# Two more seven-product pairs in the second feed-forward network, and three modulation columns moved into its first down stage

## What is computed

```python
def swiglu(h, w_gu, w_down):
    g, u = jnp.split(h @ w_gu, 2, axis=-1)
    return (jax.nn.silu(g) * u) @ w_down
...
    mod = cond @ mod_w[i] + mod_b[i]
    sh1, sc1, g1, sh2, sc2, g2, sh3, sc3, g3 = jnp.split(mod, 9, axis=-1)
    h = modulate(rms_norm(x), sh1, sc1)
    x = x + 0.5 * g1[:, None, :] * swiglu(h, ffn1_w_gu[i], ffn1_w_down[i])
...
    x = x + 0.5 * g3[:, None, :] * swiglu(h, ffn2_w_gu[i], ffn2_w_down[i])
```

## Time and profile before

| | |
|---|---|
| time, median of 3 runs | 1944.03 us (1943.16 to 1944.99) |
| profiled execution, its own time | 1943.51 us |
| its span, first to last instruction | 1941.7 us |
| busy: PE, weight loads, DVE, ACT, POOL | 98%, 86%, 73%, 47%, 11% |
| DMA, mean over the span | 136 GB/s |
| granted PE clock, mean | 0.999 |

### The profile page before, as it was taken

The page is one execution under the profiler, slowest core; times in us unless marked ns, Lnnn a source line. Parts: engine busy times, 40 slices in busy tenths (PEclk is TensorE's granted clock), DMA queues, the critical chain, the costliest instruction groups (busy, mean ns, idle before and its releaser), DMA issues.

```text
span 1941.7 us, 28004 instructions
## 1 busy us (share of the span) xinstructions
PE 1912.3 (98%) x10860; PEld 1674.0 (86%) x10860; DVE 1426.2 (73%) x2144; ACT 915.1 (47%) x1454; POOL 211.8 (11%) x245
## 2 busy tenths in 40 slices
PE   6999999999999999999999999999999999999998
PEld 5888888878888889999888998978888889899897
DVE  7664564689868798897888988876554478578485
ACT  5322222454645426446543553655565556346264
POOL 4110100016730120000011000001111000000000
PEclk9999999999999999999999999999999999999999
DMA  8665562323143583533357544333223232423232
GB/s 332 232 216 173 195 205 98 103 82 100 33 142 104 201 291 130 195 122 100 96 195 242 171 141 140 103 94 115 87 81 105 60 98 78 129 84 123 77 100 75
DMA packets 76397, 264.64 MB, mean 136 GB/s; under 512 B 8897, under 2 KB 11073, under 8 KB 76274
## 3 DMA queue, kind: packets, MB, share of 16 engines
q1 hardware_dynamic: 55296, 190.34, 30.0%
q0 software_dynamic: 20256, 72.02, 11.0%
q10 hardware_dynamic: 722, 0.61, 0.1%
HBM read 260.66 MB, written 2.13 MB: 135 GB/s over the span
## 4 chain that ended last, share of the span: by engine, by line
PE 91%; DVE 4%; issue 1%; DMA 1%; POOL 1%; ACT 1%; SPq 0%; DVEq 0%; ACTq 0%; POOLq 0%
PE bank L1827 20%; PE bank L1832 20%; PE bank L1828 20%; PE bank L1908 9%; PE bank L1907 9%; PE bank L1909 8%; DVE arena L1183 1%; PE bank L2310 1%; PE bank L2327 1%; PE bank L2242 1%; PE bank L2086 1%; DMA arena<-in_mod_t_dram 1%; DVE h_lo L1363 1%; PE bank L2088 1%; PE bank L2087 1%
## 5 line engine op out<-in xcount | busy, mean ns | idle before, releaser
L1827 PE MATMUL bank<-h_hi,whi 128*128 128x512 f32 x1008 | 400.2, 397 | 5.3 <-ACT h_hi L751 2.8
L1828 PE MATMUL bank<-h_hi,wlo 128*128 128x512 f32 x1008 | 394.3, 391 | 0.0
L1832 PE MATMUL bank<-h_lo,whi 128*128 128x512 f32 x1008 | 347.5, 391 | 2.2 <-POOL h_lo L531 2.1
L634 ACT ACTIVATE whi<-wraw 128x1024 fp32r<-128x1024 f32 x238 | 247.5, 1053 | 181.7 <-PE bank L1832 164.7
L1827 PE MATMUL bank<-hid_hi,whi 128*128 128x512 f32 (+1 forms) x856 | 328.8, 384 | 0.0
L1828 PE MATMUL bank<-hid_hi,wlo 128*128 128x512 f32 (+1 forms) x856 | 328.1, 383 | 0.0
L1832 PE MATMUL bank<-hid_lo,whi 128*128 128x512 f32 (+1 forms) x856 | 328.0, 383 | 0.0
L1096 DVE TENSOR_TENSOR wlo<-wraw,whi 128x1024 fp32r<-128x1024 f32 x224 | 271.2, 1223 | 61.6 <-ACT whi L634 61.1
L1827 PEld LDWEIGHTS bank<-h_hi,whi 128*128 128x128 f32 x1008 | 190.2, 189 | 47.6 <-issue 6.7
L1832 PEld LDWEIGHTS bank<-h_lo,whi 128*128 128x128 f32 x1008 | 189.8, 189 | 44.0 <-POOL h_lo L531 2.8
L1907 PE MATMUL bank<-h_hi,whi 128*128 128x256 f32 x800 | 226.6, 283 | 0.3 <-ACT sq L694 0.3
(11 more groups left out here) (292 smaller groups left out, 3122.9 us busy)
## 6 DMA issues: line engine op xcount, KB each, us to landing
wraw<-in_w_units_dram SPq DMA_DIRECT2D x306, 512.0 KB, 3.7
arena<-in_mod_t_dram POOLq DMA_DIRECT2D x96, 512.0 KB, 4.9
mod_tile<-in_mod_t_dram POOLq DMA_DIRECT2D x32, 512.0 KB, 4.9
wraw<-in_w_units_dram SPq DMA_DIRECT2D x32, 384.0 KB, 3.1
arena<-in_mod_t_dram SPq DMA_DIRECT2D x12, 512.0 KB, 9.2
arena<-in_w_units_dram SPq DMA_DIRECT2D x10, 512.0 KB, 4.6
xT<-in_xt_dram SPq DMA_DIRECT2D x8, 256.0 KB, 4.6
sq<-k_roots POOLq DMA_DIRECT2D x8, 256.0 KB, 3.8
```

The costliest lines, as they stand in the source:

```text
L634: act.activation(whi[:, s % RING, :, :], wraw[:, s % RING, :, :], ACT.Copy).then_inc(hi_ready, 1)
L1827: pe.matmul(dst, whi[:, w, k, :], hi_, start=first, stop=False)
L1828: pe.matmul(dst, wlo[:, w, k, :], hi_, start=False, stop=False)
L1832: return pe.matmul(dst, whi[:, s % RING, k, :], lo_, start=False, stop=last)
```

## The change

In the first third of the second network, pairs 4 and 5 become summed pairs, so that it has 18 in place of 16. The rounding and splitting of the moving blocks goes behind earlier pairs, as in the fourth network. The three columns behind pair 4 go into the first down stage, which has 23 in place of 20, three behind each output but the last, which has two.

```diff
 MOD_PLACES = [EVEN,
-              [None] * KT + [(0, 0, n) for n in (3, 3, 3, 4, 4, 4)]
-              + [(0, 1, d) for d in (0, 0, 0, 1, 1, 1, 2, 2, 2, 3, 3, 3, 4, 4, 5, 5, 6, 6, 7, 7)]
+              [None] * KT + [(0, 0, n) for n in (3, 3, 3)]
+              + [(0, 1, d) for d in (0, 0, 0, 1, 1, 1, 2, 2, 2, 3, 3, 3, 4, 4, 4, 5, 5, 5, 6, 6, 6, 7, 7)]
               + [(1, 1, d) for d in (0, 0, 0, 1, 1, 1, 2, 3, 3, 4, 5, 5, 7, 7)],
...
-PLAIN_PAIRS = {1: (6, 0, 0), 2: (6, 0, 0), 3: (4, 0, 0)}
+PLAIN_PAIRS = {1: (4, 0, 0), 2: (6, 0, 0), 3: (4, 0, 0)}
...
-        T_ROUND_AT = {1: {0: (0, 1, 2), 4: (3,)}, 2: {0: (0, 1, 2), 4: (3,)}, 3: {0: (0, 1, 2), 2: (3,)}}
-        T_SPLIT_AT = {1: {1: (0, 1), 2: (2,), 5: (3,)}, 2: {1: (0, 1), 2: (2,), 5: (3,)}, 3: {1: (0, 1, 2), 3: (3,)}}
+        T_ROUND_AT = {1: {0: (0, 1, 2), 2: (3,)}, 2: {0: (0, 1, 2), 4: (3,)}, 3: {0: (0, 1, 2), 2: (3,)}}
+        T_SPLIT_AT = {1: {1: (0, 1, 2), 3: (3,)}, 2: {1: (0, 1), 2: (2,), 5: (3,)}, 3: {1: (0, 1, 2), 3: (3,)}}
```

## The result

The change makes the kernel slower: 1956.53 us, the median of 4 runs (1955.03 to 1957.52), against 1944.34 of the kernel before beside it (1943.16 to 1944.99). The ratio is 1.0063 [1.0051, 1.0076], 12.2 us. The forecast was 1949.1 in a range from 1946.0 to 1952.5. The sign and both places were right; the size was less than half of what came.

What follows compares the result with a forecast made beforehand. TensorE, busy 98%, was taken to bound the kernel. Conversions -1.62, pair 4 stall +3.62 and down stage +3.10 gave +5.10 us: 1949.1 against 1944.03, eight in ten from 1946.0 to 1952.5.

Steps and rivals of the forecast that it cites:

- both places: TensorE gaps before the seventh product of pair 4, about 3.6 us, and of the next third's first pair, 2 to 5.
- The rule: In a summed pair, the seventh product starts at the later of 8.64 us and C + 3.35, counted from pair start.
- C: When VectorE begins the next pair's `combine`, counted from the start of the pair; from 5.29 us on it decides.
- The rival in which a late `combine` is covered: Neither stall: matmul queue or ScalarE covers it at both places; -1.62 us, 1942.4, chance 0.07.
- Term 1: Three columns beside pair 3 delay `combine` to C = 8.95, so TensorE loses 3.62 us at pair 4.
- The conversions: Pairs 4 and 5 of the second network made summed save 0.81 us each, 1.62 for two.
- The work that I costed at zero: ScalarE's copies, earlier splits and SP's weight loads for the converted pairs: no wait in TensorE's stream, cost zero.
- term 2: Down stage: three more columns and tile waits give C = 8.39 at the next third; TensorE loses 3.10 us.
- the bound without any wait for a tile: Down stage with every tile wait gone: C = 7.04 at the next third, loss 1.75 us.
- my layout: Down stage laid out by hand from tile landings: output 1 ends 1.5 us late, output 7 at 728.8, C = 8.39.
- The upper bound of 5.0: Largest down-stage loss, 5.0 us: up to 2 more for a wait of 2.11 seen in the third network.
- the clock: Rival: half clock for 3.4 us after the stalls loses 1.7 each; 1950.8 for one, 1952.5 for both, chance 0.10.

Runs made afterwards that it cites:

- e6: Changed kernel with two columns behind plain pair 2, 18 in the first down stage, six behind summed pairs of the next third; 1941.95 us, 0.9993 of the kernel before.
- e3: Changed kernel with 20 tiles of the first down stage fetching only 8 of 1,024 columns, VectorE's instructions kept; +6.7 us, 1.0033 of the kernel before.
- e8: Changed kernel with four slots used from the fourth tile on, so four tiles lie ready at the first down stage; +10.6 us, 1.0054 of the kernel before.
- e1: Changed kernel with its three columns behind plain pair 2 in place of pair 3; +7.1 us, 1.0037 of the kernel before.
- e4: Changed kernel with one of the three columns behind pair 2 and two behind pair 3; +10.2 us, 1.0055 of the kernel before.
- e7: Kernel before with only the changed column list, pairs 4 and 5 plain again; +7.1 us, 1.0035 of the kernel before.
- e2: Changed kernel with 20 columns in the first down stage, three moved behind summed pairs 2, 4, 6 of the next third; +5.7 us, 1.0031 of the kernel before.
- e5: Changed kernel with columns behind pair 2, 20 in the first down stage, three behind the next third's summed pairs; -0.1 us, 0.9998 of the kernel before.

## Why the prediction was wrong

**The rule held.** In all nine kernels, wherever C was 5.29 or more, the seventh product came 3.35 or 3.36 us after `combine`, from C = 5.33 to 11.16. The rival in which a late `combine` is covered falls.

**Term 1 held to 0.01**: C = 8.95 and the seventh product at 12.31, forecast 8.95 and 12.30. Pairs 5 to 7 carried the shift without a further stall.

**The conversions held.** The 4.61 between pair 4 and the down stage closes with -1.62, and e6, with the stalls out of the way, ends 1.7 lower. The work that I costed at zero (splits, copies, SP's loads) put no wait into PE's stream there.

**Failed: term 2, mis-sized at 3.10; it measured 5.82.** The place, the releaser and the cause were right. DVE's own work was about right too: the bound without any wait for a tile was C = 7.04, e3 measured 6.87. The waits for tiles were wrong: my layout had 8.39 - 7.04 = 1.35 us of them, there were 4.23. I had output 1 end 1.5 late and every later output run at full pace. In the trace output 1 lasts 7.75 (694.54 to 702.29) in place of 5.44, so it is 2.31 late, and the other 1.9 come at outputs 2 to 7, up to the end of the stage (0.42 at 726.34, 0.88 at 736.40). The fourth tile alone is worth more than the whole 1.35: 1.98 in e8. The upper bound of 5.0 was too low as well. It added one wait of the third network's stage, 2.11, to my own layout, though that row is a single wait and bounds no sum. Two small sums are a little off (7.67 less 0.58 is 7.09 and not 7.04, 3.10 with 2 more is 5.1 and not 5.0), which changes nothing here.

**Failed: the clock, given 0.10 and 1.7 us a stall.** It fell at both stalls and cost 2.6 each, 5.2 of the 13.04. Two things were wrong. I argued that the stalls stand between dense stretches; e1 to e4, e7 and e8 show that this does not protect. And I took the length of the one stretch that I had, 3.4 us, where two of 6.8 came. The Trainium skill (TensorE: Matmul & The Clock Gate, HAM oscillation) names idle gaps in a matmul stream as what drops the clock. By that rule this rival held, and the traces agree for each of the ten stalls of 2.45 us and more; the shortest of them is shorter than the gaps that the section speaks of, and there the measurement decides. With the earlier trace rows at hand the rival deserved far more than a tenth.

With both in place the forecast's own sum gives -1.62 + 3.63 + 2.60 + 5.82 + 2.61 = +13.0, against 12.2 between the medians. The range ended at +8.5. The larger term 2 alone, without the clock, gives +7.8 and would have stayed inside; the clock's 5.2 alone, with term 2 as forecast, gives +10.3. So the clock is the larger of the two errors.

**Open.** Stalls of one size (the seventh product of pair 4 at 12.30 or 12.31) had half clock for 6.8 us in three kernels and for 3.4 in e2. The traces sort the ten cases. Where the half clock set in while PE still waited, 0.9 to 3.4 us before the matmuls came back, it lasted 6.8 us (after at both places, e1, e3, e7, e4's second place, e8's first). Where it set in only when they ran again, 0.1 to 1.0 us after, it lasted 3.4 (e2, e4's first place, e8's second). What sets that moment stays open, and each case is one execution. No stall between 1.58 and 2.45 us was tried.

## What to carry to other kernels

Ask of each piece of filler work what stands behind it in its engine's stream: the same three columns cost 3.63 us of stall, and 2.6 of clock, ahead of `combine`, and 0.2 one pair earlier. Where a stage's transfers fill the DMA engines, sum the waits over the whole stage and not at its first shortage. And price a new stall in TensorE's stream with what the clock takes after it: here two stalls of 9.45 us together cost 14.7.

## What the runs showed of the hardware

The granted clock fell to 0.50 at each of ten single stalls of 2.45 to 5.9 us in an otherwise full matmul stream, for 3.4 or 6.8 us, and a 256-column matmul then took 0.213 in place of 0.12 us. It did not fall at stalls of 1.58 (e3), 0.98 (e2), 0.51 and 0.27 (e5) and 0.26 (e1). Where the lower clock set in matters: in e7 it began 3.4 us before the matmuls came back, and cost 1.4 in place of 2.6.
